# Bank order in PSUM, and two subtractions given to GpSimd, in a two-block transformer kernel

## The chip, the cores and the metric

The kernel runs on one core of one Trainium2 chip. Five engines work side by side: TensorE (PE in the profile, with its weight loads as PEld), VectorE (DVE), ScalarE (ACT), GpSimd (POOL) and SyncE (SP), which here only issues transfers. The metric is the time of one execution in device microseconds, the median of several runs. Each run lasts a little longer than the span that the profile shows.

## What is computed

The reference is two transformer blocks in float32 over 512 tokens of width 1024. The first block has gated linear attention, a state space layer and a feed-forward layer. The second, which holds all that the change touches, is this, cut to what matters:

```
q = (rmsnorm(q_lat) @ w_uq)      # 8 heads of 96: 64 plain, 32 rotated by position
kv = (rmsnorm(kv_lat) @ w_ukv)   # 8 heads of 64 + 64
qh, kh = concat(q_nope, rope(q_pe)), concat(k_nope, rope(k_rope) for every head)
attn = softmax(mask(qh kh^T / sqrt(96))) v        # causal, 8 heads
u = silu(layernorm(depthwise_conv(glu_a * sigmoid(glu_b), 31 taps)))
x = x + gt1 * ((sigmoid(.) * (attn @ w_o) + sigmoid(.) * (u @ w_conv_out)) @ w_out)
h = rmsnorm(x) * (1 + sc2) + sh2
x = x + gt2 * moe(h)   # 4 groups of 8 experts, width 128; one group a token, two experts in it
```

## The kernel before, in words

**Two-part products.** Each float32 operand of a large product is split into a high part (a ScalarE copy to a narrower type) and a low part (what the copy lost, a subtraction). TensorE then adds three products: high by high, high by low, low by high. The function `three` writes them. For a weight unit, 1 MB in a tile of 128 x 2048, ScalarE writes the high part (`high`, L862) and one other engine the low part (`low`, L1420). The function `next_low(name, i)` is called at a unit and splits the unit that comes *after* it in the plan. VectorE and GpSimd both call it, and the set `POOL_LOW` says which of the two does the work. `high` of a unit waits until TensorE has used the unit two before it, whose buffer it overwrites.

**Order of the work.** Each engine runs its own list of instructions in the order in which the functions `tensor`, `scalar`, `vector`, `gpsimd` and `sync` write them. Counting semaphores tie the lists together: `at(name)` is the count that a named step will reach, and `wait_ge` waits for it. An instruction that waits holds up all that stand behind it in its engine's list.

**PSUM banks.** TensorE writes into eight banks. The class `Banks` gives them out while the program is written, in TensorE's order. `take` opens a bank for a tile, `close` marks the last product into it, and a tile that is not closed keeps its bank. `fresh` (in `tensor`) takes a bank and makes TensorE wait until the last reader of the tile that had the bank before (its step `free`) is done. Before the change, a bank moves to the end of the list when it is taken, and `take` gives the first bank of the list that holds no open tile. Most tiles are closed before the next one is taken. Four kinds stay open longer: `v` in the first block, `f2` in the feed-forward layer, `pv` in attention, which gathers two heads in one bank and is taken at every even head, and the pair `y` in the mixture of experts, which gathers one block of 128 tokens over its four pairs of experts.

**The convolution and the heads.** VectorE computes the depthwise convolution in four parts of 31 steps (`convolve`, L2001), while TensorE works on the gates `ga` and `gc`. GpSimd splits the weight units of this stretch, the last of them `uq` 0, and then copies the rotated key to all eight heads (L2428). ScalarE begins with the `high` of `uq` 1 only when `convolve(3)` is done. After it VectorE splits `uq` 1, rotates heads 0 to 3 (`rope`: L2011 and L2012 read the bank, L2014 adds two tiles of SBUF), splits `kv`, rotates heads 4 to 7, splits `oa` 0 and starts on the softmax. TensorE does `uq` 1, then `kh` (the keys' heads, from unit `kv`), and then the scores of head 0, which wait for all rotations, for the keys and for GpSimd's copy.

**Attention.** For head h TensorE's list has the scores of head h+1, the transposes of the probabilities of head h (`pt`, L715), and the product with the values (`pv`). At odd heads ScalarE copies the high part of the bank `pv` and VectorE subtracts it for the low part (`attn`, L2102). That subtraction is the last reader of the bank.

**The mixture of experts.** Seven blocks of 128 tokens need twelve weight units each. GpSimd issues a gather for each of them (L2442) into six slots, as soon as the slot's last unit is split. ScalarE (L1363) and VectorE (L2249) split each unit into one of four buffers, up to three units ahead of TensorE. TensorE's order in block n is: expert units of pair 0, the last `down` unit of block n-1 (which closes its `y` pair), then the units of pair 1, and so on. VectorE scales the closed pair out of its banks (`block_out`, L2283), behind the units that it splits.

Of the kernel before, what the change touches and what calls it, by code (L numbers as in the profile page):

```python
# [66 lines left out]
for _n in range(NB):  # L67
    for _p in range(4):
        STREAM += [(_n, "ex", 2 * _p), (_n, "ex", 2 * _p + 1)]
        if _n or _p:  # L70
# [7 lines left out]
ORDER = {n: k for k, n in enumerate(SPL)}  # L78
UNIT = {p: n for n, p in enumerate(PLAN)}
POOL_LOW = {UNIT[p] for p in [("zg", i) for i in range(4)] + [("zs", 0), ("zs", 1)] + [("cin", i) for i in (1, 2, 3)]  # L80
            + [("lat", i) for i in range(3)] + [("ga", i) for i in range(4)] + [("gc", i) for i in range(4)] + [("uq", 0)]}

# [35 lines left out]
class Banks:  # L120
# [9 lines left out]
    def take(self, *tile):  # L130
        i = next(j for j in self.order if self.tenant.get(j) not in self.open)
        before = self.tenant.get(i)
        self.order.remove(i)
        self.order.append(i)
        self.tenant[i] = tile
        self.open.add(tile)
        self.place[tile] = i
        return self.banks[i][:, :], before

    def close(self, *tile):  # L140
        self.open.discard(tile)

    def at(self, *tile):
        return self.banks[self.place[tile]][:, :]


def program(nc, W, wmoe, mcst, vecs, cst, xT, wal, wgu, bc, rw, posr, posc, xslot, yslot, prep, bbar, ushuf, yshuf, out):
    ctx = ExitStack()
    with ctx:
# [28 lines left out]
        def at(*name):  # L178
            if not counted:
                return values.get(name, (pe_done, 0))  # L180
            return values[name]
# [1234 lines left out]
        def low(t, g, n):  # L1416

            t.wait_ge(*at("high", n))
            hi = wst[:, side(n), 0, :].bitcast(F32)
            g.tensor_tensor(wst[:, side(n), 1, :], ringt[:, n % RING, :], hi, SUB).then_inc(*t.sig(("low", n), ("released", n)))  # L1420
# [906 lines left out]
        def gpsimd(g):  # L2327
            q = Tally(g, pool_done, values)

            def next_low(name, i):  # L2330
                k = ORDER[UNIT[name, i]] + 1
                if k < len(SPL) and SPL[k] in POOL_LOW:
                    q.wait_ge(*q.own())
                    low(q, g, SPL[k])
# [87 lines left out]
            for name, n in (("cin", 4), ("lat", 3), ("ga", 4), ("gc", 4)):  # L2422
                for i in range(n):
                    next_low(name, i)
            q.wait_ge(*at("kpe0"))
            q.wait_ge(*at("end", "gates", "pe"))
            q.wait_ge(*q.own())
            g.tensor_copy(KH[64:96, :, :], kpe[64:96, :].unsqueeze(1).to_broadcast([32, 8, 512])).then_inc(*q.sig(("kpe_ready",)))  # L2428
            for c in range(4):
                q.wait_ge(*at("conv_sig", c))  # L2430
                q.wait_ge(*q.own())
                g.tensor_tensor(CO[:, c, :], CO[:, c, :], nrm[:, c % 2, :], MUL).then_inc(*q.sig(("conv_silu", c)))
# [133 lines left out]
        for engine in (tensor, scalar, vector, gpsimd, sync):  # L2566
            engine(Idle())
# [4 lines left out]
        block.scalar(scalar)  # L2572
        block.vector(vector)
        block.gpsimd(gpsimd)
        block.sync(sync)

# [110 lines left out]
```

## Time and profile before

| | |
|---|---|
| median of 3 runs | 1979.2 us (1975.19 to 1979.4) |
| the profiled execution | 1975.65 us, of it 1973.8 us in the span |
| TensorE busy | 1728.5 us, 88% of the span |
| VectorE, ScalarE, GpSimd busy | 1257.2, 756.8 and 323.0 us |
| mean granted TensorE clock | 0.928 of full speed |

Busy time is the time in which an engine executes instructions; waiting and the issuing of plain transfers are not in it. The whole span is cut into stages by the order above: the heads lie near 1390 us, attention runs from about 1418 to 1529 us, and the mixture of experts from about 1680 us to 1950 us.

### The profile page before, as it was taken

To read this page: it belongs to the slowest core of one execution; us is meant where nothing else is said; L and a number is where in the kernel's file an instruction comes from. 1 tells how busy PE (TensorE), PEld (TensorE's weight loads), DVE (VectorE), ACT (ScalarE), POOL (GpSimd) and SP (SyncE) were. 2 spreads that over 40 slices of the span, in tenths; PEclk is the share of its full clock that TensorE was granted. 3 is DMA by queue.
4 is the path that set the end of the run, shared out by engine and by line. 5 is a ranking of instruction groups with operands and counts; after the bars stand their busy time and mean duration, and the time that the engine had idled before them with its cause. 6 is when DMAs were issued, how large, how long until landed. Compare 5 with 4: busy or idle time off the path is not lost. (4 is left out here: it accounts for less than half of the span.)

```text
span 1973.8 us, 19274 instructions
## 1 busy us (share of the span) xinstructions
PE 1728.5 (88%) x7948; PEld 1339.4 (68%) x7948; DVE 1257.2 (64%) x1545; ACT 756.8 (38%) x938; POOL 323.0 (16%) x188
## 2 busy tenths in 40 slices
PE   4979787889899987999999969989778986999985
PEld 3858676777688864878887837767433764777764
DVE  4858556783333337643454467989776645898986
ACT  4233333233412234321232224231456225666654
POOL 1000001113300002000000014423000003544440
PEclk7989888999999998999999979989899996999998
DMA  6324212333222232444434402212100204989993
GB/s 247 116 85 157 60 38 83 119 122 108 84 87 105 86 128 85 150 151 170 164 131 152 170 22 91 86 64 86 64 0 0 86 5 172 389 335 344 346 344 135
DMA packets 59638, 264.93 MB, mean 134 GB/s; under 512 B 21648, under 2 KB 22160, under 8 KB 33056
## 3 DMA queue, kind: packets, MB, share of 16 engines
q1 hardware_dynamic: 34896, 159.56, 22.7%
q0 software_dynamic: 15184, 99.90, 13.4%
q10 hardware_dynamic: 9472, 4.26, 0.8%
q8 instruction: 62, 1.02, 0.2%
q14 instruction: 24, 0.20, 0.0%
HBM read 240.26 MB, written 23.44 MB: 134 GB/s over the span
## 5 line engine op out<-in xcount | busy, mean ns | idle before, releaser
L363 PE MATMUL bank<-h_high,wsplit 128*128 128x512 f32 x992 | 323.5, 405 | 26.9 <-POOL wsplit L1420 8.5
L1420 DVE TENSOR_TENSOR wsplit<-ring,wsplit 128x2048 fp32r<-128x2048 f32 x77 | 176.4, 2291 | 199.0 <-ACT wsplit L862 198.9
L862 ACT ACTIVATE wsplit<-ring 128x2048 fp32r<-128x2048 f32 x98 | 186.9, 1907 | 227.5 <-PE bank L363 205.5
L363 PEld LDWEIGHTS bank<-h_high,wsplit 128*128 128x128 f32 x992 | 190.4, 192 | 81.1 <-POOL wsplit L1420 9.4
L363 PE MATMUL bank<-xn_high,wsplit 128*128 128x512 f32 (+1 forms) x832 | 221.5, 354 | 25.5 <-DVE wal_low L1453 18.5
L363 PE MATMUL bank<-h_low,wsplit 128*128 128x512 f32 x496 | 199.4, 402 | 0.0
L363 PEld LDWEIGHTS bank<-xn_high,wsplit 128*128 128x128 f32 x832 | 149.2, 195 | 47.8 <-issue 19.9
L363 PE MATMUL bank<-f_high,wsplit 128*128 128x512 f32 x512 | 167.1, 407 | 4.4 <-DVE f_low L1961 4.4
L363 PE MATMUL bank<-xn_low,wsplit 128*128 128x512 f32 (+1 forms) x416 | 145.9, 351 | 0.0
L2001 DVE SCALAR_TENSOR_TENSOR conv<-conv_in,vecs,conv 128x512 f32<-128x512 f32 x120 | 140.3, 1169 | 4.3
L1420 POOL TENSOR_TENSOR wsplit<-ring,wsplit 128x2048 fp32r<-128x2048 f32 x21 | 98.8, 4706 | 171.8 <-ACT wsplit L862 171.8
L2442 POOL DMA_INDIRECT ring<-in_wmoe,indices x42 | 85.2, 2027 | 218.0 <-DVE routing L2201 135.2
L363 PEld LDWEIGHTS bank<-f_high,wsplit 128*128 128x128 f32 x512 | 99.9, 195 | 29.4 <-DVE f_low L1961 5.2
L2406 POOL TENSOR_TENSOR x<-x,z 128x512 f32<-128x512 f32 x8 | 12.8, 1594 | 599.5 <-DVE z L1899 599.5
L363 PEld LDWEIGHTS bank<-h_low,wsplit 128*128 128x128 f32 x496 | 95.6, 193 | 22.0 <-issue 0.2
L363 PE MATMUL bank<-f_low,wsplit 128*128 128x512 f32 x256 | 104.2, 407 | 0.0
L363 PE MATMUL bank<-parts,block_high 128*128 128x512 f32 x216 | 74.8, 430 | 18.4 <-DVE block_out L2283 18.4
L363 PEld LDWEIGHTS bank<-xn_low,wsplit 128*128 128x128 f32 x416 | 81.2, 195 | 11.0 <-issue 1.2
L363 PE MATMUL bank<-m_high,wsplit 128*128 128x512 f32 x256 | 81.3, 396 | 2.0 <-DVE m_low L2130 2.0
L363 PE MATMUL bank<-g_high,wsplit 128*128 128x512 f32 x256 | 80.8, 395 | 0.0
L363 PE MATMUL bank<-wsplit,block_high 128*128 128x512 f32 x232 | 76.1, 410 | 4.8 <-DVE wsplit L2249 4.8
L1958 DVE TENSOR_TENSOR norm_tmp<-norm_tmp 128x512 f32<-128x512 f32 x32 | 22.1, 690 | 71.9 <-ACT norm_tmp L1175 71.9
(470 smaller groups left out, 3368.4 us busy)
## 6 DMA issues: line engine op xcount, KB each, us to landing
ring<-in_W SPq DMA_DIRECT2D x122, 1024.0 KB, 4.9
weights_out<-prep SPq DMA_DIRECT2D x8, 864.0 KB, 5.6
prep<-weights_out_early POOLq DMA_DIRECT2D x8, 576.0 KB, 3.1
xslot<-zeros SPq DMA_DIRECT2D x7, 516.0 KB, 5.0
block<-xslot SPq DMA_DIRECT2D x7, 516.0 KB, 11.9
yslot<-block_out SPq DMA_DIRECT2D x7, 512.0 KB, 8.8
prep<-turns_early POOLq DMA_DIRECT2D x8, 288.0 KB, 2.4
x_in<-in_xT SPq DMA_DIRECT2D x4, 528.0 KB, 6.8
```

What stands on the lines that cost most here:

```text
L363: return g.matmul(o, l, r, start=first, stop=last_, skip_group_check=True)
L862: g.activation(wst[:, side(n), 0, :], ringt[:, n % RING, :], ACT.Copy).then_inc(*a.sig(("high", n)))
L1420: g.tensor_tensor(wst[:, side(n), 1, :], ringt[:, n % RING, :], hi, SUB).then_inc(*t.sig(("low", n), ("released", n)))
L1958: g.tensor_tensor(s, r, r, MUL).then_inc(*v.sig())
L2001: g.scalar_tensor_tensor(out=CO[:, c, :], in0=i, scalar=cw[:, c, k:k + 1], in1=CO[:, c, :], op0=MUL, op1=ADD).then_inc(*v.sig(("convolved",)))
L2406: g.tensor_tensor(X[:, k, :], X[:, k, :], Z[:, k, :], ADD).then_inc(*q.sig((name, "x", k)))
L2442: g.indirect_dma_start(slots[c % NS], None, wmoe, indexed(x)).then_inc(slot_landed[c % NS], 16)
```

## The change

The class `Banks` moves a bank to the end of its list when its tile is closed, not when it is taken. So `take` gives the bank that was closed longest ago. Where every tile is closed before the next is taken, both rules give the same banks. Where a tile stays open, the banks that follow are others than before.

The low parts of units `uq` 1 and `kv` go from VectorE to GpSimd. In GpSimd's list, `uq` 1 comes behind a wait for TensorE's last gate unit and ahead of the copy of the rotated key, and `kv` behind that copy. In VectorE's list the two calls of `next_low` stay and do nothing.

```
-            + [("lat", i) for i in range(3)] + ... + [("uq", 0)]}
+            + [("lat", i) for i in range(3)] + ... + [("uq", 0), ("uq", 1), ("kv", 0)]}
     def take(self, *tile):
         i = next(j for j in self.order if self.tenant.get(j) not in self.open)
         before = self.tenant.get(i)
-        self.order.remove(i)
-        self.order.append(i)
         self.tenant[i] = tile
         self.open.add(tile)
         self.place[tile] = i
     def close(self, *tile):
         self.open.discard(tile)
+        i = self.place[tile]
+        self.order.remove(i)
+        self.order.append(i)
             for name, n in (("cin", 4), ("lat", 3), ("ga", 4), ("gc", 4)):
                 for i in range(n):
                     next_low(name, i)
+            q.wait_ge(*at("end", "gates", "pe"))
+            next_low("uq", 0)
             q.wait_ge(*at("kpe0"))
-            q.wait_ge(*at("end", "gates", "pe"))
             q.wait_ge(*q.own())
             g.tensor_copy(KH[64:96, :, :], kpe[64:96, :].unsqueeze(1).to_broadcast([32, 8, 512])).then_inc(...)
+            next_low("uq", 1)
```

The rest of the kernel is the same, the transfers and their order too.

## Rows read from the trace of the kernel before

**Rows 1.** The page, part 1: busy time, share of the span, instructions.

```profile
PE 1728.5 (88%) x7948; PEld 1339.4 (68%) x7948; DVE 1257.2 (64%) x1545; ACT 756.8 (38%) x938; POOL 323.0 (16%) x188
```

**Rows 2.** TensorE's waits from 1684 us on: total us, times, longest.

```profile
PE bank L363 <- DVE block_out L2283: 18.4, 6, 3.1
```

**Rows 3.** Windows by expert block: length, busy us, PEclk, DMA share, GB/s.

```profile
1684.20:1719.96 35.76, 32.70 (x148) 26.24 (x148) 34.58 (x32) 26.17 (x22) 18.39 (x13) 0.98 0.96 384
1719.96:1761.20 41.24, 38.17 (x161) 30.50 (x161) 35.32 (x33) 26.16 (x22) 18.30 (x13) 0.93 0.88 331
1761.20:1799.84 38.64, 35.58 (x160) 28.52 (x160) 35.31 (x33) 26.16 (x22) 18.28 (x13) 1.00 0.94 353
1799.84:1840.02 40.18, 37.11 (x161) 29.61 (x161) 35.33 (x33) 26.16 (x22) 18.30 (x13) 0.96 0.91 341
...
1878.65:1918.20 39.55, 37.14 (x160) 29.69 (x160) 34.67 (x32) 26.14 (x22) 17.91 (x12) 0.96 0.92 339
```

**Rows 4.** VectorE's waits in one expert block, 1761.20 to 1799.84 us.

```profile
DVE parts L2249 <- ACT parts L1363: 1.7, 2, 1.4
DVE hidden_low L2262 <- ACT hidden_high L1378: 1.0, 1, 1.0
```

**Rows 5.** Timeline of VectorE at that block's end: start, duration, instruction.

```profile
1799.10 1.28 DVE L2283 TENSOR_TENSOR block_out<-bank,rows 128x512 f32<-128x512 f32 x2
1800.30 2.28 DVE L2249 TENSOR_TENSOR wsplit<-slot,wsplit 128x2048 fp32r<-128x2048 f32 x1
```

**Rows 6.** Timeline of TensorE and VectorE in attention; in brackets the wait before.

```profile
1458.77 3.70 PE L363 MATMUL bank<-norm_tmp,cst 128*128 128x512 f32 x8 [1.41 <-DVE attn L2102]
...
1485.01 5.40 PE L363 MATMUL bank<-kh,qh 96*128 96x512 f32 x8 [1.95 <-DVE attn L2102]
...
1508.38 3.70 PE L363 MATMUL bank<-kh,qh 96*128 96x512 f32 x8 [1.80 <-DVE attn L2102]
...
1509.63 2.69 DVE L2082 TENSOR_SCALAR probs<-probs,small 128x512 f32<-128x512 f32 x4
```

**Rows 7.** Timeline of four engines at the heads.

```profile
1370.05 3.87 POOL L2428 COPY kh<-k_pe 32x4096 f32<-32x4096 f32 x1 [4.08 <-PE bank L363]
...
1390.24 1.91 ACT L862 ACTIVATE wsplit<-ring 128x2048 fp32r<-128x2048 f32 x1 [19.70 <-DVE conv L2001]
...
1392.25 2.29 DVE L1420 TENSOR_TENSOR wsplit<-ring,wsplit 128x2048 fp32r<-128x2048 f32 x1 [2.04 <-ACT wsplit L862]
...
1394.60 0.79 PE L363 MATMUL bank<-q_high,wsplit 128*128 128x512 f32 x1 [16.29 <-DVE wsplit L1420]
...
1405.98 0.45 PE L363 MATMUL bank<-kv_high,wsplit 128*64 128x512 f32 x1 [1.18 <-DVE wsplit L1420]
...
1419.30 0.69 DVE L2069 SCALAR_TENSOR_TENSOR probs<-bank,mask 128x512 f32<-128x512 f32 x1 [1.98 <-PE bank L363]
```

**Rows 8.** VectorE's rotations grouped by line, 1394 to 1415 us.

```profile
L2011 DVE TENSOR_TENSOR rope_tmp<-bank,rope_table 32x512 f32<-32x512 f32 x8 | 5.5, 689 | 1.1
L2014 DVE TENSOR_TENSOR qh<-rope_tmp 32x512 f32<-32x512 f32 x8 | 5.5, 683 | 0.3
```

**Rows 9.** Chain of waits in the convolution: start, duration, one step each.

```profile
1369.70 0.76 DVE conv L2001
1370.49 3.98 DVE conv L2001
```

**Rows 10.** The page, part 5: GpSimd's subtractions of a weight unit.

```profile
L1420 POOL TENSOR_TENSOR wsplit<-ring,wsplit 128x2048 fp32r<-128x2048 f32 x21 | 98.8, 4706 | 171.8 <-ACT wsplit L862 171.8
```

**Rows 11.** Timeline of GpSimd and VectorE where both work at once.

```profile
1499.21 1.27 POOL L2432 TENSOR_TENSOR conv<-conv,norm_tmp 128x512 f32<-128x512 f32 x1 [10.95 <-ACT norm_tmp L1299]
...
1499.75 0.69 DVE L2072 TENSOR_REDUCE small<-probs 128x1 f32<-128x512 f32 x1
...
520.08 6.38 POOL L2395 TENSOR_TENSOR o_low<-o,o_high 128x512 fp32r<-128x512 f32 x4 [16.84 <-ACT o_high L1102]
...
520.55 4.75 DVE L1847 TENSOR_TENSOR o_low<-o,o_high 128x512 fp32r<-128x512 f32 x3 [0.34 <-ACT o_high L1102]
```

More of the change, by code:

```diff
@@ L80 @@
 POOL_LOW = {UNIT[p] for p in [("zg", i) for i in range(4)] + [("zs", 0), ("zs", 1)] + [("cin", i) for i in (1, 2, 3)]
-            + [("lat", i) for i in range(3)] + [("ga", i) for i in range(4)] + [("gc", i) for i in range(4)] + [("uq", 0)]}
+            + [("lat", i) for i in range(3)] + [("ga", i) for i in range(4)] + [("gc", i) for i in range(4)] + [("uq", 0), ("uq", 1), ("kv", 0)]}
 def side(n):
@@ L132, in take @@
         before = self.tenant.get(i)
-        self.order.remove(i)
-        self.order.append(i)
         self.tenant[i] = tile
@@ L141, in close @@
         self.open.discard(tile)
+        i = self.place[tile]
+        self.order.remove(i)
+        self.order.append(i)
     def at(self, *tile):
@@ L2424, in gpsimd @@
                     next_low(name, i)
+            q.wait_ge(*at("end", "gates", "pe"))
+            next_low("uq", 0)
             q.wait_ge(*at("kpe0"))
-            q.wait_ge(*at("end", "gates", "pe"))
             q.wait_ge(*q.own())
             g.tensor_copy(KH[64:96, :, :], kpe[64:96, :].unsqueeze(1).to_broadcast([32, 8, 512])).then_inc(*q.sig(("kpe_ready",)))
+            next_low("uq", 1)
             for c in range(4):
```

## The prediction

> **What bounds the kernel now.** I read the page's busy times first: TensorE is busy for 88% of the span, the next engine, VectorE, for 64% [rows 1]. So TensorE's idle time is what can be won, and only in the stages that the two edits touch. I then went to TensorE's waits stage by stage.
>
> In the mixture of experts TensorE waits six times for `block_out`, 18.4 us in all, 3.1 at most [rows 2]. It is the only wait of weight in that stage. The windows, cut at those waits, show how near the other engines are [rows 3]: in the cleanest block (38.64 us, clock 1.00) TensorE works 35.58 us, VectorE 35.31, and the transfers take 0.94 of the time. The same windows show a second price: after three of the waits the clock of the block is 0.93 to 0.96, and TensorE's busy time 38.17, 37.11 and 37.14 us for the same 160 products.
>
> In attention, the third view shows three waits of 1.41, 1.95 and 1.80 us for the subtraction on the `pv` bank [rows 6]. At the heads, VectorE's convolution is what everyone waits for: ScalarE 19.70 us, TensorE 16.29 us, which ends with the low part of `uq` 1 [rows 7].
>
> **Edit 1, the bank order.** I wrote down the takes and closes in TensorE's order and applied both rules. Up to `cin` 2 the banks are the same. `cin` 3 to 5 get other ones, whose tenants were closed five or more takes earlier. Behind that two places matter.
>
> *Experts.* Before, the first unit of pair 1 in block n gets the bank of `y`(n-1), closed just ahead of it, and must wait for `block_out`. With the new rule it gets the bank of `xt`(n), the next the other half's. Every new predecessor there is a `th`, `gu`, `xt` or an old `y` tile, at least four takes back, whose reader TensorE has already had to wait for through another step. So no wait takes the place of this one in PSUM. What is removed: 6 waits, 18.4 us [rows 2]. With them should go the slow clock behind them: (38.17 - 35.58) + (37.11 - 35.58) + (37.14 - 35.58) = 5.7 us [rows 3]. Upper bound 24.1 us.
>
> What is late next? When TensorE stands, VectorE is three units ahead: its next split (1800.30) follows `block_out` (1799.10) [rows 5], and it is of the unit that TensorE wants three units later, some 9 us on (35.58/12 = 2.97 each). So TensorE can go on at once. Over a whole block VectorE must keep up: it waits 2.7 us in 38.64 for ScalarE, which waits for TensorE [rows 4], so these waits shrink as TensorE moves earlier, to a floor of 38.64 - 2.7 = 35.9 us. The transfers: 0.94 x 38.64 = 36.3 us at 353 GB/s, but block 0 moved 384 GB/s at a share of 0.96 and lasted 35.76 with a wait in it [rows 3]; 353 x 38.64 / 384 = 35.5 us. Three resources thus end at 35.6 to 36.3, and four buffers between them let little be lost. I take a block of 36.1 us. That gains 38.6 - 36.1 = 2.5 in each of six, 15.0, and the clock's 5.7, less 0.7 for the last block's drain: 20 us. Bounds: 0 (another engine takes all of it) and 24.1. I lean to the upper end because block 0 shows the flow without a wait.
>
> *Attention.* The wait of 1.41 stands ahead of scores that VectorE wants at once: gained, 1.4. The second, 1.95, is followed by 5.40 us for eight products which take 3.70 at the two other places, so 1.95 + 1.70 in sum [rows 6]; but the transposes behind these scores also need probabilities that VectorE finishes at its own pace, so I count only as much as at the first, 1.4. The third, 1.80: TensorE's scores would end near 1510.3 and the probabilities end at 1512.3 [rows 6], so I count 0.2. Sum 3.0; bounds 1 and 6.9 (all three and the slow clock). `oa` 3, which also followed a `pv` bank, showed no wait.
>
> **Edit 2, the low parts.** Four terms on the path through the heads, in order.
>
> 1. The copy of the rotated key ran at 1370.05 for 3.87 us, and the convolution step beside it took 3.98 in place of 0.76 [rows 7, 9]. GpSimd's copy now stands behind the low part of `uq` 1, and that behind its high part, which ScalarE starts only when the convolution is done. So it leaves the convolution: 3.2 us earlier for everything behind.
> 2. The low part of `uq` 1: GpSimd takes 4.7 us where VectorE took 2.3 [rows 7, 10]: 2.4 later. TensorE starts at 1393.8, not 1394.6.
> 3. The low part of `kv`. GpSimd's list is then: `uq` 1 from 1389.0, copy 3.9, `kv` 4.7. Both engines' SBUF work excludes the other's [rows 9], but they take turns: four subtractions of GpSimd took 6.38 us and three of VectorE, in the same time, 4.75 [rows 11]. With two turns of 0.69 between them, `kv` is ready near 1403.7. TensorE ends `uq` 1 near 1404.0 (0.8 earlier than now) and need not wait the 1.18 that it does [rows 7]. Gain so far 2.0.
> 4. The rotations, 8 heads at three operations of 0.69, some 2.2 with gaps [rows 8]. GpSimd now works from 1389.0 to 1403.7 beside them. An operation of VectorE with one SBUF source was not held up by GpSimd's (0.69 at 1499.75, inside GpSimd's 1.27) [rows 11]. So the two that read the bank go on, and the third, with two SBUF sources, waits for GpSimd's end each time: about one head per GpSimd instruction. Three heads are done at 1404.4, the other five by 1415.7. The last `kh` product needs the bank of head 7 at about 1415.0, so it ends at 1416.4, 1.0 earlier than now. VectorE's next split (2.3) ends at 1418.0, and the softmax starts at about 1418.1, not 1419.30 [rows 7].
>
> The Trainium skill ("SBUF — State Buffer", section "SBUF: two separate sides") says that the port pair of the two engines is an exclusive lock for a whole instruction, and that of VectorE's operations only those in a two-port mode or with two SBUF inputs need it. The trace agrees (0.69 and 3.98), and the sum by the rule is the one above.
>
> Edit 2 in sum: 1.1 us gained. Bounds: 2.0 gained (no hold-up at all) and 5 lost: if GpSimd shuts out all rotations until 1403.7, eight heads end at 1421.5 instead of 1415.7, and 1.1 becomes a loss of about 4.7. Scores 0 wait for them, and behind those the whole of attention. No transfer moves; the ring slots of `uq` 1 and `kv` come free 1 to 2 us earlier.
>
> **Sum.** 20 + 3.0 + 1.1 = 24 us. The profiled execution took 1975.65 us (span 1973.8): it would be 1951.6. The median of the runs shown is 1979.2, 3.6 above it, so on its scale 1955.
>
> **The rivals.**
> *A. The wait turns into another.* VectorE, ScalarE's copies or the gathers hold TensorE at 37.5 us or so a block: for it speak a transfer share of 0.94 and VectorE's 35.31 of 38.64; against it block 0's 384 GB/s. Gain 6 x 1.1 + half of the clock's 5.7 = 9.5, and 4: 1966.
> *B. GpSimd shuts VectorE out at the heads.* For it: 3.98 and `uq` 1 on the path. Against it: the turns at 520 us. Loss 4.7 in place of a gain of 1.1: 1961.
> *C. The experts drop to the low clock.* If TensorE, always just behind VectorE, stops for short times at many units, and each stop brings half clock for the next unit (2.4 us more, as 38.17 - 35.58), then from ten units of 84 on the gain of 24 is gone; at 20 units it is 1955 + 48 = 2003, slower than before. Against it: all stretches without a wait stand at 1.00.
> *D. The edits do nothing measurable*, because the chain from the gathers sets the experts' time and only attention moves: 3 to 4 us, 1976.
>
> **How the numbers follow.** Forecast 0.66, A 0.18, B 0.08, C 0.03, D 0.05. The forecast's own range is 1950 to 1961. With A and B, and 2 us for the runs' scatter, the range is 1948 to 1969. The measurement can tell about 0.2% (4 us) from no change. Faster by more than that: forecast, A, B and a part of D, 0.93. Within it: 0.04. Slower: 0.03.
>
> **What would show it.** Right: TensorE's waits from the first expert block on hold no `block_out`; the blocks last 35.6 to 36.6 us with the clock near 1.00; no wait for `attn` in attention; the convolution has no step of 3.98 after the gates; TensorE's first product of `uq` 1 comes some 0.8 us sooner, GpSimd shows three operations in a row, and L2014 is stretched for three heads. Wrong: TensorE waits for `parts` or `wsplit` in the experts (A), the first softmax step starts later than before relative to the convolution's start (B), a clock under 0.93 there (C).

## The result, and the profile after

| | before | after |
|---|---|---|
| median | 1977.2 us (4 runs) | 1947.33 us (4 runs: 1951.24, 1952.48, 1943.41, 1943.36) |
| profiled execution | 1975.65 us | 1951.24 us |
| span, mean granted clock | 1973.8 us, 0.928 | 1949.4 us, 0.934 |

The ratio is 0.9849 with a 95% interval of 0.9819 to 0.9878: 29.9 us faster. The forecast was 1955 us and a gain of 24, its range 1948 to 1969. The direction and the mechanism were right, but the median lies 0.7 us below the range. The two profiled executions differ by 24.4 us.

The first view is the page's part 1 of the kernel after, which answers to [rows 1].

```profile
PE 1723.1 (88%) x7948; PEld 1333.2 (68%) x7948; DVE 1251.1 (64%) x1543; ACT 757.0 (39%) x938; POOL 335.4 (17%) x190
```

The same 7948 products take 5.4 us less, since fewer of them run at half clock. VectorE has two instructions fewer, GpSimd two more. The other 19 us are idle time of TensorE.

TensorE's waits in the experts (1682 to 1930 us) and in attention (1419 to 1532 us) answer to [rows 2] and to the brackets of [rows 6].

```profile
PE bank L364 <- DVE hidden_low L2263: 3.8, 7, 0.9
```

```profile
PE bank L364 <- ACT probs_t L1283: 5.6, 7, 0.8
PE bank L716 <- DVE conv L2108: 4.7, 1, 4.7
PE bank L716 <- DVE probs L2083: 2.6, 3, 1.1
PE bank L364 <- DVE probs L2070: 0.9, 1, 0.9
```

`block_out` and `attn` are gone from both. What is new is small: 0.5 us a block for `hidden_low`, which before cost 0.9 us once, and in attention one stop more for `probs` (before: 2, of 2.0 us in all). The other waits of attention were there before, the same to 0.2 us. The windows by expert block answer to [rows 3] (same columns); the last two rows are the five blocks from the first `block_out` to the sixth, and what follows them.

```profile
1717.62:1753.65 36.03, 35.55 (x162) 28.51 (x161) 35.19 (x34) 26.18 (x22) 18.21 (x12) 1.00 0.95 379
1753.65:1789.67 36.02, 35.54 (x162) 28.50 (x161) 35.19 (x34) 26.17 (x22) 18.19 (x12) 1.00 0.97 381
...
1717.60:1897.76 180.16, 177.77 (x802) 142.50 (x801) 175.95 (x162) 130.89 (x110) 91.01 (x60) 1.00 0.96 379
1897.76:1925.50 27.74, 26.33 (x117) 20.76 (x116) 22.49 (x24) 13.76 (x13) 4.01 (x2) 1.00 0.41 153
```

A block now takes 36.0 us, 35.55 of them TensorE's own work, at full clock; the same bytes go through in less time, 379 GB/s in place of 331 to 353.

I cut every profiled execution at the starts of the same instructions of VectorE. The convolution runs from its first step to its last, the heads from there to the first softmax step, attention from there to the last `attn`, mixing 2 (the product with `w_out` behind attention) from the last gating of the convolution's branch to the last update of `x`, and the experts, with the routing ahead of them, from the copy of the router's logits to the last `block_out`. The stages in which anything moved, in us:

| kernel | clock | convolution | heads | attention | mixing 2 | experts |
|---|---|---|---|---|---|---|
| before | 0.928 | 167.9 | 29.8 | 109.9 | 42.8 | 311.8 |
| after | 0.934 | 165.0 | 31.1 | 108.1 | 44.3 | 288.6 |
| `e1_again` | 0.932 | 165.0 | 31.1 | 108.2 | 44.3 | 288.6 |
| `e11_again` | 0.936 | 164.7 | 31.2 | 107.7 | 42.7 | 287.7 |
| `e12_look` | 0.934 | 165.0 | 31.2 | 108.0 | 42.8 | 287.7 |
| `e2_banks` | 0.931 | 168.2 | 29.8 | 105.6 | 42.8 | 288.8 |
| `e3_lows` | 0.930 | 165.1 | 31.1 | 110.1 | 42.8 | 310.5 |
| `e4_copy_early` | 0.930 | 168.2 | 30.7 | 108.0 | 42.8 | 288.9 |
| `e5_y_alone` | 0.929 | 168.3 | 29.8 | 112.5 | 44.4 | 287.4 |
| `e6_copy_late` | 0.935 | 164.7 | 30.8 | 109.6 | 42.8 | 287.9 |
| `e7_out_late` | 0.934 | 165.0 | 31.2 | 107.9 | 42.7 | 294.4 |
| `e8_both_late` | 0.931 | 165.1 | 30.8 | 108.1 | 44.3 | 298.6 |
| `e9_load_first` | 0.934 | 165.0 | 31.2 | 108.0 | 42.8 | 285.4 |
| `e10_best` | 0.932 | 165.1 | 30.8 | 108.0 | 44.3 | 286.6 |

From before to after: experts -23.2, convolution -2.9, heads +1.3, attention -1.8, mixing 2 +1.5, and 0.8 more in all the rest. That is the 24.4 of the two profiled executions, within rounding.

From the first `block_out` to the last alone it is 231.6 us before and 230.4 in `e3_lows`, and 208.5 to 208.6 in after, `e1_again`, `e2_banks`, `e4_copy_early`, `e5_y_alone`, `e6_copy_late`, `e11_again` and `e12_look`. What else the column of the experts differs by, 0.9 us between executions of the changed kernel, lies ahead of the first `block_out`.

### The profile page after: what moved, and what is told of

Its sections match the earlier page's. It is cut to its first block and busy times, and to the rows that moved or that the text cites. A ratio compares the mean times of both kernels' runs of the same rounds, so it can differ in the third digit from the quotient of the medians.

```text
span 1949.4 us, 19283 instructions
## 1 busy us (share of the span) xinstructions
PE 1723.1 (88%) x7948; PEld 1333.2 (68%) x7948; DVE 1251.1 (64%) x1543; ACT 757.0 (39%) x938; POOL 335.4 (17%) x190
## 5 line engine op out<-in xcount | busy, mean ns | idle before, releaser
L1421 DVE TENSOR_TENSOR wsplit<-ring,wsplit 128x2048 fp32r<-128x2048 f32 x75 | 171.8, 2291 | 200.5 <-ACT wsplit L863 200.5
L1421 POOL TENSOR_TENSOR wsplit<-ring,wsplit 128x2048 fp32r<-128x2048 f32 x23 | 108.1, 4701 | 196.4 <-ACT wsplit L863 196.3
L364 PE MATMUL bank<-parts,block_high 128*128 128x512 f32 x216 | 68.9, 400 | 0.0
```

Source lines behind the costliest of these rows:

```text
L364: return g.matmul(o, l, r, start=first, stop=last_, skip_group_check=True)
```

## The experiments

Each group of four is held against executions of before on its own chip: experiments 1 to 4 against 1978.05 us (17 runs, 1972.2 to 1982.57), 5 to 8 against 1977.18 (11 runs, 1971.83 to 1980.5), 9 to 12 against 1977.78 (11 runs, 1968.81 to 1983.88). Differences between kernels of different groups are the less certain for it.

**1. The changed kernel again** (`e1_again`), no edit.

> The changed kernel once more, against the kernel before on one chip. Theory T (the steps are sized right, and what the medians gained beyond the forecast is TensorE's granted clock, which differs from execution to execution outside the stages that the change touches): five rounds give a gain between 22 and 32 us; in the profile the experts last 243 to 244 us from the first full-speed product to the last, the blocks 36.0 us, and runs that are faster than others of the same kernel have a higher granted clock. Rival S (a term is too small: the change gains some 30 us and the first profile was an unlucky draw): the gain is 28 to 32 us, and the new profile shows experts, attention or heads shorter than the first did by 5 us or more in sum.

1951.68 us (1951.14 to 1952.1), ratio 0.987 (0.9849 to 0.989): 26.4 us faster. The stages repeat those of after within 0.1 us.

**2. The bank order alone** (`e2_banks`). Only the four moved lines of `Banks`:

```
-        self.order.remove(i)      # in take
-        self.order.append(i)
+        i = self.place[tile]      # in close
+        self.order.remove(i)
+        self.order.append(i)
```

> The bank order alone, all low parts as before. T: the experts gain 22 to 23 us (six waits for block_out and the slow clock behind them gone, blocks 36.0 us), attention 2 to 3 us, the heads 0: 23 to 26 us in all. Rival S: 28 to 30 us. If the two edits help each other (attention starts with VectorE behind), it is less than the change without its 1.1 to 1.4 us.

1950.57 us (1947.84 to 1956.05), ratio 0.9867 (0.9846 to 0.9889): 27.5 us faster, as much as the whole change beside it (26.4). As far as these runs can tell, the bank order is the whole gain.

**3. The low parts alone** (`e3_lows`). Only `POOL_LOW` and GpSimd's new order, old `Banks`.

> The low parts of uq 1 and kv by GpSimd alone, bank order as before. T: 1 to 2 us faster (softmax starts 1.3 us sooner after the heads), which five rounds may not tell from nothing; TensorE's waits for block_out and attn are back. Rival B (GpSimd shuts VectorE out): 3 to 5 us slower. Rival S: 5 us or more faster.

1976.41 us (12 runs, 1969.84 to 1979.5), ratio 0.9993 (0.9981 to 1.0005): not to be told from no change. With the old bank order the waits are back (TensorE, from 1684 us on, then 1419 to 1532 us; first and second fence):

```profile
PE bank L363 <- DVE block_out L2283: 18.4, 6, 3.1
PE bank L363 <- DVE hidden_low L2262: 0.9, 1, 0.9
```

```profile
PE bank L363 <- DVE attn L2102: 5.2, 3, 2.0
```

**4. The copy of the key early again** (`e4_copy_early`). The changed kernel, but GpSimd's list has `next_low("uq", 0)` behind the copy, not ahead of it:

```
             q.wait_ge(*at("end", "gates", "pe"))
-            next_low("uq", 0)
             ...
             g.tensor_copy(KH[64:96, :, :], ...)
+            next_low("uq", 0)
             next_low("uq", 1)
```

> The change with GpSimd's copy of the rotated key back at its old place, ahead of the low part of uq 1, so beside the convolution. T: the convolution has its step of 3.98 us again and everything behind comes 3.2 us later, of which 0.7 to 1.5 us come back, since GpSimd then has 3.9 us less to do beside the rotations: 1.7 to 2.5 us slower than the change. If the copy costs the path nothing, no difference, and the gain at the heads was from the low parts themselves.

1953.16 us (1952.83 to 1954.41), ratio 0.9879 (0.9859 to 0.99); 1.5 us slower than `e1_again`, whose slowest execution (1952.1) lies under the fastest here (1952.83). I expected 1.7 to 2.5. The convolution takes 168.2 again, the heads 30.7. GpSimd's timeline (start, duration, instruction, in brackets the idle time before):

```profile
1370.52 3.87 POOL L2429 COPY kh<-k_pe 32x4096 f32<-32x4096 f32 x1 [4.09 <-PE bank L364]
1393.56 9.50 POOL L1421 TENSOR_TENSOR wsplit<-ring,wsplit 128x2048 fp32r<-128x2048 f32 x2 [19.17 <-ACT wsplit L863]
```

The copy stands where it stood in [rows 7] and costs the convolution the same 3.2 us. The term is shown by putting this one cost back.

**5. The new rule for `y` alone** (`e5_y_alone`). On the kernel before, a bank moves at its close if its tile is a `y`, at its taking if it is any other:

```
+        if tile[0] != "y":        # in take
             self.order.remove(i)
             self.order.append(i)
+        if tile[0] == "y":        # in close
+            i = self.place[tile]
+            self.order.remove(i)
+            self.order.append(i)
```

> The kernel before, with the new order only for the y tiles of the experts (all other banks still move when they are taken). T: the experts gain the same 22 to 23 us as with the full change, attention and heads nothing: the time is 22 to 23 us below the kernel before. Rival (part of the gain is from the other banks of the expert stage or from attention's order): less than 18 us.

1954.94 us (1954.15 to 1957.59), ratio 0.9888 (0.9873 to 0.9903): 22.2 us faster. The experts gain all they gain in after (287.4; 208.6 from the first `block_out` to the last), while in attention the three waits for `attn` stay, 5.2 us. So the `y` pair's place in the order is the whole of the experts' gain, 23.0 us between the first `block_out` and the last. How the medians' 27.5 us split between experts and attention is less sure than 22.2 and the rest: this profiled execution, the slowest of the four, took 2.6 us more than before in attention, where its waits are those of before, and 1.6 more in mixing 2.

**6. The low part of `uq` 1 back on VectorE** (`e6_copy_late`), with the copy behind it:

```
- ... [("uq", 0), ("uq", 1), ("kv", 0)]}
+ ... [("uq", 0), ("kv", 0)]}
             q.wait_ge(*at("kpe0"))
+            q.wait_ge(*at("low", UNIT["uq", 1]))
             q.wait_ge(*q.own())
             g.tensor_copy(KH[64:96, :, :], ...)
```

> The change, but the low part of uq 1 is VectorE's again; GpSimd copies the rotated key only when that is done (so still behind the convolution), then splits kv. T: TensorE's first product of uq 1 comes 2.3 us sooner than in the change, and GpSimd has two long operations beside the rotations, not three: softmax starts some 2 us sooner, 2 us off the time. If VectorE's place there is what counts (it is the one that is late at the heads), the gain is under 0.5.

1949.57 us (1942.58 to 1950.79), ratio 0.985 (0.9831 to 0.987). TensorE starts `uq` 1 at 1391.50, 2.75 earlier than in after, but the stage becomes only 0.3 us shorter (31.1 to 30.8). TensorE's waits at the heads say why:

```profile
PE bank L364 <- DVE wsplit L1421: 13.1, 1, 13.1
PE bank L364 <- DVE rope_tmp L2013: 1.9, 3, 0.7
```

The products of `kh` now wait for the banks that the rotations read. VectorE's rotations set the end of the stage, and TensorE's early start is handed back to them. I expected 2 us off; the expectation's other case, that VectorE's place is what counts and the gain is under 0.5, is what came.

**7. `block_out` later** (`e7_out_late`). With the bank no longer waited for, `block_out` need not be early. VectorE does it behind the next block's first turn of `hidden`:

```
                     if pr or n:
                         turn_hidden(*before)
+                    if n and pr == 1:
+                        block_out(n - 1)
                     ...
-                        if before[1] == 3:
-                            block_out(before[0])
```

> The change, with block_out one step later in VectorE's list, behind the low part of the hidden units of pair 0 (only possible now that no product waits for it). T: in the changed kernel TensorE still waits about 0.45 us a block for that low part, which stands behind block_out (1.28 us); without it the blocks last 35.6 us and not 36.02: 2 to 3 us off the time, with VectorE's 35.2 us of work as the next bound. Rival (transfers or VectorE bound the block at 36.0): no difference.

1956.92 us (1950.74 to 1964.35), ratio 0.9899 (0.9879 to 0.992). I expected 2 to 3 us less than the changed kernel and got some 6 more (1950.9 is the median of its 14 executions). The wait for `hidden_low` is nearly gone as planned, but TensorE has another (waits, 1682 to 1940 us):

```profile
PE bank L799 <- DMA block<-xslot: 8.3, 5, 2.4
PE bank L364 <- DVE hidden_low L2263: 0.9, 1, 0.9
```

SyncE's list has the load of the next block's rows behind the store of `y`, and the store waits for `block_out`. What I delayed on VectorE I delayed on a queue that I hadn't followed. SyncE's timeline, first of after, then of this kernel:

```profile
1718.93 0.32 SPq L2563 DMA_DIRECT2D yslot<-block_out  x1
1719.29 0.49 SPq L2551 DMA_DIRECT2D block<-xslot  x1
```

```profile
1722.14 0.32 SPq L2563 DMA_DIRECT2D yslot<-block_out  x1
1722.50 0.43 SPq L2551 DMA_DIRECT2D block<-xslot  x1
```

The load goes out 3.2 us later, 0.4 us behind the store in both.

**8. Both late edits** (`e8_both_late`): those of 6 and 7 together.

> The edits of the last two together. T: 4 to 5 us off the change's time, their sum, since one acts at the heads and one in the experts. If the granted clock answers to the later phase, the sum misses by some microseconds either way.

1959.02 us (1954.35 to 1962.54), ratio 0.9907 (0.9892 to 0.9922), experts 298.6. I expected 4 to 5 us less than the changed kernel. The wait of 7 for the rows is here too, 9.8 us of it: a second sight of the mechanism, and no more.

**9. The load ahead of the store** (`e9_load_first`): 7 with SyncE's list turned round.

```
             for n in range(NB):
-                if 0 < n < NB - 1:
-                    load_block(n + 1)
+                if n < NB - 2:
+                    load_block(n + 2)
                 s.wait_ge(*at("y_out", n))
                 g.dma_start(yslot[...], ...)
```

> The change, with block_out one step later and, in SyncE's list, the load of block n+2 ahead of the store of block n (it needs only the hidden units of block n, which are done). Theory L (the later block_out lost because the next block's load stands behind its store in SyncE's list: in the run before, it was issued at 1722.50 us against 1719.29 in the change, and TensorE waited 8.3 us in five times for it): those waits are gone and the 0.45 us a block as well, so blocks of 35.6 us, 2 to 3 us below the change. Rival (transfers are the bound at 36 us): the blocks stay at 36.0 or more and the time at the change's, whatever the order.

1948.29 us (1946.14 to 1950.28), ratio 0.9851 (0.9824 to 0.9879), where I expected 2 to 3 us less than the changed kernel. The wait for the rows is gone and the experts take 285.4, the least of all. The load now leaves 14.5 us ahead of the store (SyncE's timeline, first fence), the waits of TensorE in the stage are 2.1 us in all, and the block is TensorE's own work to 0.06 us (waits, then window; second and third fence):

```profile
1742.36 0.32 SPq L2551 DMA_DIRECT2D block<-xslot  x1
1756.88 0.32 SPq L2563 DMA_DIRECT2D yslot<-block_out  x1
```

```profile
PE bank L820 <- DVE hidden L2276: 1.2, 1, 1.2
PE bank L364 <- DVE hidden_low L2263: 0.9, 1, 0.9
```

```profile
1719.99:1755.58 35.59, 35.53 (x162) 28.48 (x161) 35.01 (x34) 26.17 (x23) 19.67 (x13) 1.00 0.98 374
```

**10. The best of both** (`e10_best`): 9 with the edit of 6.

> As the kernel before this in the list, and the low part of uq 1 by VectorE again, with GpSimd's copy behind it. If L holds: 4 us below the change, 30 us below the kernel before. If the copy's place helps nothing by itself (softmax started only 0.7 us sooner in that run than in the change): as the kernel before this in the list, within 1 us.

1948.23 us (1939.06 to 1950.48), ratio 0.9845 (0.9817 to 0.9873).

**11 and 12. The changed kernel beside them** (`e11_again`, and `e12_look`, a single execution).

> The changed kernel a third time, as the measure for the two above on the same chip, and for how its time scatters. T: a gain of 25 to 28 us over the kernel before, with single executions 8 us apart and the granted clock higher in the faster ones; its profile differs from the first two in the length of attention (108.1 us from the first softmax step to the last low part) or in the mixing behind it, not in the experts (36.0 us a block).

> The changed kernel once more, for one profile: if the granted clock moves by itself, the experts and the heads have the same lengths as before to 0.3 us, and what differs between this execution and the others lies in stages with waits of TensorE ahead of them (the first 200 us, attention, the mixing, the routing).

`e11_again`: 1949.39 us (1948.39 to 1951.12), ratio 0.9862 (0.9835 to 0.9889); `e12_look`: 1950.32 us. So 9 and 10 lie only 1.1 us under the change, within what these runs can tell, though their stage is 1.1 to 3.2 us shorter. They beat the kernel before clearly, and the changed one not measurably.

## Why the prediction was right, and where it was wrong

**The experts: the mechanism right, the term too small.** This is the term of the sum that failed: 20 us forecast, 23.2 measured. "What is removed: 6 waits, 18.4 us": gone with the bank order (2, 5), back without it (3). "I take a block of 36.1 us": 36.02 to 36.04. The limit was chosen between three resources that ended at 35.6 to 36.3. Experiment 9 shows TensorE's own 35.5 as the lowest of them reached, so neither VectorE's "floor" of 35.9 nor the transfers' 36.3 is one: a block there takes 35.59. (VectorE's view for that block has a third wait for ScalarE, 0.3 us for `wsplit`, that the 35.9 leaves out.) What after has above 35.5 is the wait for `hidden_low`. Rival A is out: no wait of 1.1 a block came in the place of the old one. Rival C is out: the clock is 1.00 in every block (its price, 38.17 - 35.58, is 2.6 and not 2.4). Rival D is out: the experts did set the gain.

The term was 20 us and came out at 23.2 in the profiled pair (23.2 to 24.1 over the changed kernel's four profiled executions). Cut at the sixth `block_out`, the windows show where the rest was. Those of before, to be held against the last two of after:

```profile
1719.20:1918.10 198.90, 183.58 (x800) 146.85 (x800) 176.59 (x161) 130.78 (x110) 91.47 (x60) 0.97 0.92 343
1918.10:1950.10 32.00, 30.31 (x127) 24.16 (x128) 22.72 (x24) 13.75 (x13) 1.86 (x2) 0.95 0.34 133
```

Five blocks: 198.90 - 180.16 = 18.7, where the forecast's own numbers give 5 x 2.5 + 5.7 = 18.2. The last: 32.00 - 27.74 = 4.3, where they give 2.5 - 0.7 = 1.8. The step that failed there is "With them should go the slow clock behind them", counted from three windows of which the last ended at 1918.20 [rows 3], and with it the 2.5 and the 0.7 for the last block. Behind the sixth wait was a fourth slow stretch that no window held. TensorE's timeline of before, 12 products of one unit in a row:

```profile
1918.85 0.73 PE L363 MATMUL bank<-parts,block_high 128*128 128x512 f32 x2 [3.06 <-DVE block_out L2283]
...
1920.44 1.06 PE L363 MATMUL bank<-parts,block_high 128*128 128x512 f32 x2
...
1923.01 0.63 PE L819 MATMUL bank<-cst,hidden 128*128 128x128 f32 x2
```

They take 4.16 us (1918.85 to 1923.01); three such products take 0.70 at full clock (1924.23 to 1924.93 in the same timeline), so twelve 2.8: 1.4 lost. The wait's 3.06 and these 1.4 make 4.5, the 4.3 within 0.2. The 0.7 that I took off for the drain didn't show: behind the sixth `block_out` the only stop of TensorE in after is one of 0.48 for `hidden_low`.

**Attention: the mechanism right, the term too large.** All three waits for `attn` are gone, 5.2 us. I counted 3.0 for them and measured 1.7 to 2.2 in the executions of the changed kernel. One reading was wrong: the wait of 1.41 doesn't stand "ahead of scores". The row in [rows 6] is of eight products of `norm_tmp` with a constant, and the scores come behind them, at 1462.31. The size held all the same: from the product `pv` ahead of it (1453.71) to those eight it was 5.06 us, and in after it is 3.57 (1452.77 to 1456.34), 1.5 less where I counted 1.4. At the two later places TensorE's timeline of after shows both ways in which the time is given back:

```profile
1484.37 0.72 PE L716 MATMUL bank<-cst,probs 128*128 128x128 f32 x2
1486.17 3.43 PE L716 MATMUL bank<-cst,probs 128*128 128x128 f32 x14 [1.08 <-DVE probs L2083]
...
1509.26 3.07 PE L716 MATMUL bank<-cst,probs 128*128 128x128 f32 x14 [1.07 <-DVE probs L2083]
...
1513.11 5.50 PE L364 MATMUL bank<-probs_t,v 128*64 128x512 f32 x8 [0.78 <-ACT probs_t L1283]
```

TensorE comes to the transposes before VectorE has the probabilities (1.08, 1.07), as the forecast feared at the second wait. (The stop of 1.51 for them that before has at 1520.08 is gone.) And behind such a stop products run at half clock: 5.50 us for eight which take 3.62 at 1490.38, and 3.43 for 14 transposes which with the bank order alone took 2.03:

```profile
1488.91 2.03 PE L716 MATMUL bank<-cst,probs 128*128 128x128 f32 x14 [1.07 <-DVE probs L2083]
```

Where in this stage the clock falls differs between executions with the same waits, and it moves the stage as much as the edit does. Windows of the stage for before, after, `e2_banks`, `e5_y_alone` and `e11_again` (columns as in [rows 3]):

```profile
1419.30:1529.20 109.90, 91.18 (x297) 44.24 (x296) 76.28 (x152) 62.93 (x125) 5.42 (x4) 0.94 0.02 8
1417.90:1526.00 108.10, 93.76 (x297) 45.14 (x296) 76.28 (x153) 63.23 (x125) 5.42 (x4) 0.92 0.03 10
1421.60:1527.20 105.60, 91.09 (x297) 43.40 (x296) 76.22 (x153) 62.87 (x125) 5.43 (x4) 0.94 0.02 9
1421.00:1533.50 112.50, 93.86 (x297) 44.06 (x296) 76.16 (x152) 62.77 (x125) 5.43 (x4) 0.91 0.02 8
1418.10:1525.80 107.70, 91.54 (x297) 43.70 (x296) 76.26 (x152) 62.90 (x124) 5.42 (x4) 0.94 0.03 10
```

From before to after TensorE's idle time falls by 4.4 us (109.90 - 91.18 against 108.10 - 93.76), and the same 297 products take 2.6 longer: that is the 1.8. With the bank order alone the products take 91.09. But the clock is not all: in `e11_again` they take 91.54, and the stage is only 0.4 us shorter than in after, since there TensorE waits 4.1 us for `probs` and not 2.6. I had a stage in which half clock was already visible in [rows 6] and gave it no term in the sum, only in the upper bound. For `e2_banks` and `e5_y_alone` these are one execution each.

**The heads: right almost instruction by instruction, and worth nothing that the medians show.** "3.2 us earlier" for the convolution: 2.9, and shown by 4. "Three heads" held up: yes. GpSimd's timeline of after, then VectorE's of the third operation of a rotation:

```profile
1389.68 4.51 POOL L1421 TENSOR_TENSOR wsplit<-ring,wsplit 128x2048 fp32r<-128x2048 f32 x1 [23.92 <-ACT wsplit L863]
...
1394.35 3.86 POOL L2430 COPY kh<-k_pe 32x4096 f32<-32x4096 f32 x1 [0.15 <-POOL wsplit L1421]
...
1398.28 4.92 POOL L1421 TENSOR_TENSOR wsplit<-ring,wsplit 128x2048 fp32r<-128x2048 f32 x1
```

```profile
1390.91 0.69 DVE L2013 TENSOR_TENSOR rope_tmp<-bank,rope_table 32x512 f32<-32x512 f32 x1
1391.64 3.10 DVE L2015 TENSOR_TENSOR qh<-rope_tmp 32x512 f32<-32x512 f32 x1
...
1396.33 2.42 DVE L2015 TENSOR_TENSOR qh<-rope_tmp 32x512 f32<-32x512 f32 x1
...
1400.33 3.42 DVE L2015 TENSOR_TENSOR qh<-rope_tmp 32x512 f32<-32x512 f32 x1
...
1405.33 0.68 DVE L2015 TENSOR_TENSOR qh<-rope_tmp 32x512 f32<-32x512 f32 x1
...
1417.95 0.69 DVE L2070 SCALAR_TENSOR_TENSOR probs<-bank,mask 128x512 f32<-128x512 f32 x1 [0.54 <-PE bank L364]
```

The operation that reads the bank (L2013) keeps its 0.69 inside GpSimd's 4.51; the one with two SBUF sources ends just behind each of GpSimd's three. The softmax starts at 1417.95, the forecast said 1418.1. TensorE's first product of `uq` 1 came at 1394.25, 0.35 us earlier than before where I had 0.8, since ScalarE's copy behind the convolution started at 1387.60, 2.6 us sooner than in [rows 7] and not 3.2. Rival B, in which all rotations wait, is refuted. The Trainium skill ("SBUF — State Buffer", section "SBUF: two separate sides") has the port pair of the two engines as a lock held for a whole instruction, needed by VectorE for two SBUF inputs but not for one; 0.69 and 3.10 side by side agree with it.

The net of convolution and heads is 1.6 us where I forecast 1.1. But as a whole kernel edit 2 measured 1.6 us (experiment 3, interval from 3.8 faster to 1.0 slower), and on top of the bank order nothing (1951.68 against 1950.57). In the profiled executions what it saves at the heads is lost again in attention (105.6 with the bank order alone, 107.7 to 108.2 with both) and, in some, in mixing 2. With one execution of the bank order alone, whether that is the edit's doing or chance is not shown. In mixing 2 two products take 1.05 us at 1579.06 in after, and 0.63 at 1579.13 in `e12_look`, which is the same program.

**The sum and its range.** Term by term, forecast and profiled pair: experts 20 and 23.2, attention 3.0 and 1.8, heads 1.1 and 1.6, mixing 2 and the rest 0 and -2.3. The sum, 24 against 24.4, is closer than its terms, and that is luck: the experts' 3.2 too little stand against 3.5 too much in attention and in what I had at 0. What put the median outside the range is the gain and two steps more. "The median of the runs shown is 1979.2, 3.6 above it": three draws were taken for the kernel's level. On the result's own median of before, 1977.2, the same range would be 1946 to 1967, and 1947.33 inside it. All 43 executions of before have a median of 1977.8 and run from 1968.81 to 1983.88. And "2 us for the runs' scatter": the 15 us of those 43 show that a median of four can lie further off. The 14 executions of the changed kernel have a median of 1950.9; against 1977.8 that is a gain of 26.9, and the four of the result are their two fastest, 1943.36 and 1943.41, and two near 1952. On the pooled numbers the forecast's 1955 is some 4 too high: 1.4 from the level of before, 2.9 from the gain. The 2.9 is about the size of what the experts' term missed, but the profiled pair, with 24.4, doesn't show it, and where the pooled gain exceeds that pair's stays open. Where the two fastest executions won their 8 us over the rest is open too: neither was profiled.

## What to carry to other kernels

When banks or buffers are given out in a fixed order, order them by when their tenant is *closed*: the bank of a long-lived tile that has just been closed is the worst one to give next, since its new owner pays both the reader's time and the slow clock behind the stop (here 18.4 us of waits and some 7 of clock). Before an operation is moved later on one engine, follow its result into every queue, plain loads that stand behind its store included; and where a stage shows half-clock stretches, give them a term with both signs, because an edit of 1 or 2 us there can be paid back by where they fall.

## What the runs showed of the hardware that I had not expected

The same program takes times 15 us apart, and the time follows the mean granted clock: among the 39 executions of before that ran beside the experiments the time falls by 1.1 us for each 0.001 of clock (correlation -0.83), from 1983.88 us at 0.926 to 1968.81 at 0.934; the changed kernel's lie at 0.98 us for 0.001, with 1952.48 at 0.933 and 1943.36 at 0.940. Inside one program, mixing 2 has its half-clock stretch in two of four profiled executions of the changed kernel (44.3 against 42.7 us), with the same 1.75 us of idle time in front of it in both kinds. What decides it, the runs don't tell; nor do they show that the clock is the cause of all the scatter, only that the two go together.

Where VectorE and GpSimd held each other up at the heads, VectorE paid and GpSimd hardly did. Each of VectorE's three long operations ended 0.55 us behind the end of GpSimd's instruction beside it. GpSimd's subtractions took 4.51 and 4.92 us, within the 4.50 to 5.12 of the 21 of before (4.71 on the mean [rows 10]), and its copy 3.86 where it was 3.87 beside the convolution.
